# Even layer: attention work in turns beside the in2 linear, the five-tap convolution on its tiles

## The chip, the cores and the metric

One NeuronCore of a Trainium2 chip runs the whole program. The metric is device microseconds for one execution; the median of three runs of the kernel before is 4711.61 us (4707.65 to 4717.33). PE is the tensor engine, DVE the vector engine, ACT the scalar engine, POOL is GpSimd, and SP issues most of the DMAs.

## The reference

The program is a block of two parts over 256 tokens of 2048 features. The first part (a convolution and state-space mixer, a cross attention, an expert layer) is not touched. The second part has an even and an odd layer; the change is in the even one:

```
def even_layer(x, mem, rel_table, norm_g, w_in, conv_w, ..., w_out, lambda_init):
    h = rms_norm_2(x, norm_g) @ w_in
    gq, gk, gv, gb, ga, gg, dq, dk, dv, dg, mq, mg = split_cols(h, EV_SPLITS)
    y = concatenate([
        gdn_branch(gq, gk, gv, gb, ga, gg, conv_w, a_log, dt_bias, gdn_gain),
        diff_attention(dq, dk, dv, dg, rel_table, dq_gain, dk_gain, lam, subln, lambda_init),
        memory_attention(mq, mg, mem, mem_norm, mem_w_kv, mem_qn, mem_kn)])
    return x + y @ w_out
```

- `gdn_branch`: gq, gk and gv (1024 features each) go through a centred convolution of five taps along the tokens and a silu; q and k are normed a head; gb and ga (16 columns each, "the narrow product") give the gates; then a gated delta rule in both directions, a norm and a silu gate.
- `diff_attention`: 8 heads, each with two maps of 64 features. Both maps are normed for q and k, scored with a relative bias, and softmaxed; the second, times a learned lambda, is taken off the first; the result meets dv (128 a head), is normed with `subln` and gated by silu(dg).
- `memory_attention`: 4 heads of 128 over 256 memory rows with normed q and k and a silu gate.

None of the branches depends on another. All is fp32.

## The kernel before

Activations lie feature-major: a tile is 128 features by 256 tokens, x is 16 such chunks. A `Stage` is one block of code for all engines, with its own tiles and semaphores; between stages the engines meet. When few semaphores are free a stage first clears the used ones (`MOST_SEMS` is the reserve).

Weights stream through one ring of four slots for the whole program (`WeightRing`): a piece is 512 KB, 256 input rows by 512 output columns. SP issues piece g when piece g - 4 has been split; the last act of a linear in SP's queue is to load the next linear's first four. `linear` (line 413) goes over tiles of 512 outputs, and in a tile over 8 pieces. For each piece ACT makes the leading part of the fp32 weights (line 394), DVE the trailing part (line 399), and PE does 24 matmuls of 256 columns: leading weights by both parts of the features, trailing weights by the leading part (line 494). ACT may only write a slot of the leading tile when PE has freed it four pieces ago. After a tile, DVE evicts its 4 x 256 columns (lines 544 to 556). The loop over tiles is a hardware loop where a tile has 8 pieces; out2 and out3, of 10 pieces a tile, are written out.

The even layer (line 2336) runs in this order, stage after stage: linear att2 (64 pieces: q, k, gate of the difference attention, q and gate of the memory attention), linear dv2 (16 pieces), `narrow` (line 1892), `write_bias_rows` (line 1939: 8 rows of the bias go to memory), head norms of the memory keys and queries (`head_norm`, line 644: squares on ACT, sums on PE, inverse root on ACT and DVE, spreading over the partitions on PE, product on DVE), memory attention (`attention`, line 1155), head norms of the difference queries and keys, `load_bias` (line 1964: the bias is read back from memory as 8 falling grids of 384 columns and turned by PE), `difference_weight` (line 2305: lambda), difference attention, its head norm and gate, then linear in2 (64 pieces, into `proj`, 32 chunks), and the delta rule (line 2285), which begins with `centered_conv` (line 2004). That one has POOL copy the 24 chunks into a tile with zero columns at both ends, five DVE instructions a chunk (one a tap, four chunks side by side), and a silu on ACT for every four chunks. The memory keys and values were made in the first part and are fetched during att2.

Of the kernel before, what the change touches and what calls it, by code (L numbers as in the profile page):

```python
# [9 lines left out]
P = 128  # L10
# [30 lines left out]
def pieces_of_two_pi():  # L41
# [34 lines left out]
    ("upto", 2 * P), ("before", 2 * P), ("levels", 2 * LEVELS * P), ("round", 1),  # L76
# [26 lines left out]
class Stage:  # L103
# [3 lines left out]
    MOST_SEMS = 40  # L107
# [305 lines left out]
def linear(k, ring, src, dst, residual=False, tokens=False, parts=None, norm=None, fetch=None):  # L413
# [10 lines left out]
    with Stage(nc, f"lin_{name}") as s:  # L424
# [12 lines left out]
        if norm and tokens:  # L437
            col, turned, upright = s.sb("col", [P, TILES]), s.sem("turned"), s.sem("upright")

# [11 lines left out]
        def tile_list(eng):  # L451

            yield 0, 0
            if summing and tiles > 1:
                yield 1, 1
                yield from tile_pairs(eng, tiles, 2) if loops else ((n, n % 2) for n in range(2, tiles))
                return
            yield from tile_pairs(eng, tiles, 1) if loops else ((n, n % 2) for n in range(1, tiles))

        with s.block() as block:  # L460
            @block.sync
            def _(sp):
                if fetch:
                    for to, found in fetch[1]:
                        sp.dma_start(to[:], found).then_inc(fetch[0], 16)
                ring.rest(sp, job)

            @block.tensor
            def _(pe):
                if norm and tokens:  # L470
                    for t in range(TILES):
                        mm = nc.tensor.transpose(acc[:, 1, t, 0:P], norm.scale[:, t * P:(t + 1) * P], k.const("ident"))
                    mm.then_inc(turned, 1)
                for n, half in tile_list(pe):

                    pe.wait_ge(taken, n + 1)
                    for c in range(per):
# [19 lines left out]
                        if first_tile(n) and summing:  # L497
# [4 lines left out]
                            mm.then_inc(summed, 1)  # L502

            @block.scalar
            def _(act):
                for n, _ in tile_list(act):
                    for c in range(per):
# [21 lines left out]
                        if second_tile(n) and summing and c == min(1, per - 1):  # L529
                            inverse.on_scalar(act)  # L530

            @block.vector
            def _(dve):
                v = nc.vector

                def take(n, half):
# [12 lines left out]
                    out = dst[:, bass.ds(n * 4, 4) if not isinstance(n, int) else slice(n * 4, n * 4 + 4)]  # L549
                    if residual:  # L550
# [14 lines left out]
                if summing:  # L565
                    ch = Chain(dve, step)
                for n, half in tile_list(dve):
                    for c in range(per):
# [20 lines left out]
                        if not first_tile(n) and c == min(3 if summing else 1, per - 1):  # L589
                            take(n - 1, 1 - half)  # L590
                take(tiles - 1, (tiles - 1) % 2)

# [734 lines left out]

def cross_attention(k, ring, h, y, key, value):
# [674 lines left out]
def centered_conv(k, x):  # L2004

    nc = k.nc

    chunks, pad, side = 24, (GDN_CONV - 1) // 2, 4
    with Stage(nc, "conv5") as s:
        wide = s.sb("wide", [P, chunks, SEQ + 2 * pad])  # L2010
        step, done, moved = s.sem("step"), s.sem("done"), s.sem("moved")
        weights = k.col("ev_conv")
        with s.block() as block:
            @block.scalar
            def _(act):
                with act.Fori(0, chunks // side) as i:
                    act.wait_ge(done, i + 1)
                    here = x[:, bass.ds(i * side, side)]
                    nc.scalar.activation(here, here, ACT.Silu)

            @block.gpsimd
            def _(pool):
                nc.gpsimd.memset(wide[:, :, 0:pad], 0.0)
                nc.gpsimd.memset(wide[:, :, pad + SEQ:], 0.0)
                for c in range(0, chunks, side):
                    nc.gpsimd.tensor_copy(wide[:, c:c + side, pad:pad + SEQ], x[:, c:c + side]).then_inc(moved, 1)

            @block.vector
            def _(dve):
                ch = Chain(dve, step)  # L2030
                for i in ch.loop(chunks // side, GDN_CONV):

                    dve.wait_ge(moved, i + 1)
                    for tap in range(GDN_CONV):
                        for c in range(side):
                            here = x[:, bass.ds(i * side + c, 1)]
# [661 lines left out]
```

## Time and profile before

| | us |
|---|---|
| median of three runs | 4711.61 |
| profiled execution, time | 4704.41 |
| profiled execution, span | 4702.8 |
| small stages between dv2 and in2 | 218.2 |
| in2 linear | 191.3 |
| five-tap convolution | 62.2 |

A row of a timeline gives the start and the duration in us, engine, line, what is written from what, the number of instructions merged in it, and in brackets the idle time before it with what ended it. A matmul of fp32 operands stands as two records, one of the split parts as one; a record's printed duration overlaps the next one, so its pace is the distance of starts, or a merged row's duration by its count. The granted clock is a share of 2.4 GHz: 1.00 is that, 0.50 is 1.2 GHz, and a value between is a mean over a stretch that had both.

### The profile page before, as it was taken

The numbers are of one execution on the slowest core, as the hardware profiler recorded it, in microseconds if no ns is written. First come the engines' busy times: TensorE is split into PE (matmuls) and PEld (weight loads), VectorE is DVE, ScalarE is ACT, GpSimd is POOL, SyncE is SP. The second block draws the span as 40 slices with busy tenths as digits, with TensorE's granted clock in tenths as the row PEclk, the third lists the DMA queues.
The fourth block names the chain that finished last, engine by engine and source line by source line (L and its number), as shares of the span: only waits on it lengthen the run. The fifth ranks groups of instructions, "written<-read, shape, count | busy, mean of one in ns | idle before, by whom it ended". The sixth has DMA issues, their size and how long they took to land. (4 is left out here: it accounts for less than half of the span.)

```text
span 4702.8 us, 67077 instructions
## 1 busy us (share of the span) xinstructions
PE 4060.8 (86%) x24872; PEld 3592.4 (76%) x24872; DVE 2591.6 (55%) x3882; ACT 1634.9 (35%) x2075; POOL 53.1 (1%) x99
## 2 busy tenths in 40 slices
PE   7878789988589999999999989866946879997679
PEld 7864489974478888888888879746946779997569
DVE  4578654448865655655655655334455554543534
ACT  3214333330244444444444433223311123431333
POOL 0002000000000000000000000000000000000000
PEclk9989899989899999999999999867968989998779
DMA  6333344533356656656656535302510004553104
GB/s 214 120 101 121 103 148 140 158 107 117 125 196 209 206 184 213 205 187 209 205 189 209 187 131 188 126 14 68 183 36 1 0 32 163 180 182 111 37 25 164
DMA packets 181929, 645.74 MB, mean 137 GB/s; under 512 B 24744, under 2 KB 27048, under 8 KB 179888
## 3 DMA queue, kind: packets, MB, share of 16 engines
q1 hardware_dynamic: 173328, 620.56, 39.9%
q0 software_dynamic: 2016, 19.92, 1.1%
q8 instruction: 169, 2.77, 0.2%
q10 hardware_dynamic: 6336, 1.84, 0.2%
q14 instruction: 80, 0.66, 0.0%
HBM read 621.26 MB, written 20.99 MB: 137 GB/s over the span
## 5 line engine op out<-in xcount | busy, mean ns | idle before, releaser
L1813 DVE TENSOR_TENSOR dense_weights_trailing<-weight_ring,dense_weights_leading 128x1024 fp32r<-128x1024 f32 x512 | 624.2, 1225 | 557.2 <-ACT dense_weights_leading L1777 556.4
L1777 ACT ACTIVATE dense_weights_leading<-weight_ring 128x1024 fp32r<-128x1024 f32 x512 | 538.5, 1058 | 679.8 <-PE dense_down L1767 351.5
L1745 PE MATMUL dense_up<-pe_parts,dense_weights_leading 128*128 128x512 f32 x2048 | 720.0, 399 | 21.1 <-DVE dense_weights_trailing L1813 14.7
L1767 PE MATMUL dense_down<-dense_weights_leading,dense_act_parts 128*128 128x512 f32 x2048 | 630.4, 389 | 0.0
L1745 PE MATMUL dense_up<-pe_parts,dense_weights_trailing 128*128 128x256 f32 x2048 | 552.6, 280 | 0.0
L494 PE MATMUL lin_in_acc<-lin_in_parts,lin_in_weights_leading 128*128 128x256 f32 x2432 | 445.6, 286 | 30.5 <-DVE lin_in_weights_trailing L399 30.5
L1745 PEld LDWEIGHTS dense_up<-pe_parts,dense_weights_leading 128*128 128x128 f32 x2048 | 378.8, 188 | 113.5 <-issue 18.9
L1767 PEld LDWEIGHTS dense_down<-dense_weights_leading,dense_act_parts 128*128 128x128 f32 x2048 | 384.5, 188 | 79.2
L399 DVE TENSOR_TENSOR lin_in_weights_trailing<-weight_ring,lin_in_weights_leading 128x1024 fp32r<-128x1024 f32 x216 | 263.2, 1224 | 266.2 <-ACT lin_in_weights_leading L394 266.2
L494 PEld LDWEIGHTS lin_in_acc<-lin_in_parts,lin_in_weights_leading 128*128 128x128 f32 x2432 | 383.9, 194 | 31.5 <-issue 30.6
L1767 PE MATMUL dense_down<-dense_weights_trailing,dense_act_parts 128*128 128x512 f32 x1024 | 398.3, 389 | 0.0
L1745 PEld LDWEIGHTS dense_up<-pe_parts,dense_weights_trailing 128*128 128x128 f32 x2048 | 387.1, 189 | 10.1
L494 PE MATMUL lin_out_acc<-lin_out_parts,lin_out_weights_leading 128*128 128x256 f32 x1792 | 327.7, 286 | 26.1 <-DVE lin_out_weights_trailing L399 26.1
L394 ACT ACTIVATE lin_in_weights_leading<-weight_ring 128x1024 fp32r<-128x1024 f32 x216 | 227.6, 1057 | 343.3 <-PE lin_in_acc L494 341.3
L494 PE MATMUL lin_in_acc<-lin_in_parts,lin_in_weights_trailing 128*128 128x256 f32 x1216 | 346.0, 285 | 0.0
L494 PEld LDWEIGHTS lin_out_acc<-lin_out_parts,lin_out_weights_leading 128*128 128x128 f32 x1792 | 283.7, 195 | 27.1 <-issue 27.1
L494 PE MATMUL lin_out_acc<-lin_out_parts,lin_out_weights_trailing 128*128 128x256 f32 x896 | 255.7, 285 | 0.0
L494 PEld LDWEIGHTS lin_in_acc<-lin_in_parts,lin_in_weights_trailing 128*128 128x128 f32 x1216 | 235.3, 194 | 0.0
L1767 PEld LDWEIGHTS dense_down<-dense_weights_trailing,dense_act_parts 128*128 128x128 f32 x1024 | 192.2, 188 | 40.2
L494 PE MATMUL lin_att_acc<-ev_parts,lin_att_weights_leading 128*128 128x256 f32 x1024 | 188.1, 286 | 14.5 <-DVE lin_att_weights_trailing L399 14.5
L399 DVE TENSOR_TENSOR lin_out_weights_trailing<-weight_ring,lin_out_weights_leading 128x1024 fp32r<-128x1024 f32 x112 | 136.4, 1224 | 114.5 <-ACT lin_out_weights_leading L394 114.5
L494 PE MATMUL lin_in_acc<-ev_parts,lin_in_weights_leading 128*128 128x256 f32 x1024 | 187.0, 286 | 10.3 <-DVE lin_in_weights_trailing L399 10.3
(600 smaller groups left out, 6780.6 us busy)
## 6 DMA issues: line engine op xcount, KB each, us to landing
weight_ring<-in_w_experts SPq DMA_DIRECT2D x512, 512.0 KB, 4.0
weight_ring<-in_w_in SPq DMA_DIRECT2D x216, 512.0 KB, 4.1
weight_ring<-in_w_out SPq DMA_DIRECT2D x112, 512.0 KB, 4.3
weight_ring<-in_w_att SPq DMA_DIRECT2D x64, 512.0 KB, 4.3
weight_ring<-in_w_key SPq DMA_DIRECT2D x32, 512.0 KB, 3.5
weight_ring<-in_w_value SPq DMA_DIRECT2D x32, 512.0 KB, 3.5
weight_ring<-in_w_query SPq DMA_DIRECT2D x32, 512.0 KB, 4.2
weight_ring<-in_w_o SPq DMA_DIRECT2D x32, 512.0 KB, 4.3
```

The lines of the kernel that those rows point to most:

```text
L394: self.nc.scalar.activation(leading, x, ACT.Copy).then_inc(self.led, 1)
L399: return self.nc.vector.tensor_tensor(trailing, x, leading.bitcast(F32), ALU.subtract)
L494: mm = nc.tensor.matmul(acc[:, half, sub], still, moving, start=begin and m == 0, stop=end and m == 2, skip_group_check=not tokens)
L1745: mm = nc.tensor.matmul(to, still, moving, start=begin and m == 0, stop=end and m == 1)
L1767: mm = nc.tensor.matmul(down[:, bank, t], still, moving, start=begin and m == 0, stop=end and m == 2)
L1777: nc.scalar.activation(ring.leading[:, b], ring.ring[:, b], ACT.Copy).then_inc(split_led, 1)
L1813: v.tensor_tensor(ring.trailing[:, b], ring.ring[:, b], ring.leading[:, b].bitcast(F32), ALU.subtract).then_inc(ring.split, 1)
```

## The change

In words:
- The stages between dv2 and in2 are gone but for `write_bias_rows` and `difference_weight`, which now follow each other. Their work is in a class `EvenBeside`, which `linear` takes as `beside` for in2. Each engine has a generator of turns. After each of the 64 pieces PE takes one turn; ACT and DVE, which split four pieces ahead, take turn i after their part of piece i + 4. The loop over tiles is written out.
- PE's turns in order: narrow product, bias grids and sums of squares (turns 1 to 6), spreading of 12 groups of two chunks (9 to 14), memory attention (15 to 23), difference attention (24 to 51, three turns a head), the last norm (53, 54, 57, 58).
- DVE has a second generator, `finish`: the convolution of a tile of in2, one tap (four instructions) after each of five pieces in eight, from piece 12. The first six tiles are evicted into 4 chunks of x and the convolution writes `proj`; the edge columns are left out instead of padded. ACT's silus of these tiles are its last turns.
- x is needed for room (bias, raw tile): it goes to memory in two DMAs of 1 MB during dv2 and comes back during the delta rule's second head norm.
- In turns, a norm's scale is spread a head at a time from one column broadcast over 128 or 64 columns, not from a tile of broadcast copies.
- The bias is read during in2 by one DMA of SP's queue ahead of the ring's; the narrow weights are fetched in att2 on SP's queue, not on ACT's in their own stage.
- The masks of the delta rule (2 x 7 x 128 columns) are no longer part of the constants loaded at the start; they are loaded in the delta rule's first head norm, and the second waits for them.
- `MOST_SEMS` goes from 40 to 60. The columns of att2 stand in another order.

The diff, cut to its core (the classes that are new are quoted where the order or a wait matters):

```diff
-    MOST_SEMS = 40
+    MOST_SEMS = 60
...
 def linear(..., fetch=None, beside=None):
+        other = beside(s) if beside else None
...
+            if other:
+                yield from ((n, n % 2) for n in range(1, tiles))
+                return
...  (SP)
+                if other:
+                    other.on_sync(sp)
                 ring.rest(sp, job)
...  (PE, after each piece)
+                        if other:
+                            next(turns, None)
...  (ACT, after each piece)
+                        if other and n * per + c >= slots:
+                            next(turns, None)
...  (DVE, after each piece)
+                        if other:
+                            if not first_tile(n) and c == slots:
+                                take(n - 1, 1 - half)
+                            if n * per + c >= slots:
+                                next(turns, None)
+                            if n * per + c >= slots + per:
+                                next(finishing, None)
...
+class NormsBeside:
+    def square(self, act, g):
+        if g >= 2:
+            act.wait_ge(self.summed, g - 1)
+        activation(self.sq[:, g % 2], self.groups[g][0], ACT.Square).then_inc(self.squared, 1)
+    def spread_out(self, pe, g):
+        if g >= 2:
+            pe.wait_ge(self.applied, g - 1)
+        for c, t, at in self.columns(g):
+            for h in range(heads):
+                mm = matmul(self.rows[h * wide:(h + 1) * wide, g % 2, ...],
+                            self.scale[:, at + h:at + h + 1].to_broadcast([P, wide]), ident)
...
+class AttentionBeside:
+        self.turn_lag, self.turn_part = {1: (3, 0), 2: (1, 1), 3: (1, 1)}[step]
+        self.value_lag = {1: 5, 2: 2, 3: 2}[step]
+    def turns(self):
+        for i in range(self.heads + self.value_lag):
+            for part in range(self.step if i < self.heads + self.value_lag - 1 else 1):
+                yield i, part
...  (PE)
+        for i, part in self.turns():
+            if i < self.heads and part < maps:
+                scores(i * maps + part)        # waits for most() of two units before
+            if part == self.turn_part and 0 <= i - self.turn_lag < self.heads:
+                turn(i - self.turn_lag)        # waits for normalize()
+            if part == 0 and 0 <= i - self.value_lag:
+                values(i - self.value_lag)     # waits for ACT's copy
+            yield
...  (ACT: raise_unit in parts 1 and 2, copy in part 1)
...  (DVE)
+            if i < self.heads and part < maps:
+                most(i * maps + part)
+            elif i < self.heads and part == self.step - 1:
+                for c in range(maps):
+                    normalize(i * maps + c)
+            if part == 0 and 0 <= i - self.value_lag:
+                take(i - self.value_lag)
...
+class EvenBeside:
+    CONVOLVED = 6
+    def finish(self, dve, taken):
+        for n in range(self.CONVOLVED):
+            dve.wait_ge(taken, n + 3)
+            for tap in (pad, *(x for x in range(GDN_CONV) if x != pad)):
+                for j in range(4):
+                    if tap == pad:
+                        ins = v.tensor_scalar(self.proj[:, c], self.raw[:, j], w, None, ALU.mult)
+                    else:
+                        ins = v.scalar_tensor_tensor(out=self.proj[:, c, to], in0=self.raw[:, j, seen], ...)
+                ch.then(ins)
+                yield
+            yield from idle(3)
...
-def centered_conv(k, x):
...
 def delta_rule(k, proj, ba, spare, out, back):
-        centered_conv(k, proj)
-        head_norm(k, q, 8, 1, 1, GDN_DK ** -0.5)
-        head_norm(k, kk, 8, 1, 1, 1.0)
+        head_norm(k, q, ..., fetch=(masks_here, [... k.args["levels"] in two halves ...]))
+        head_norm(k, kk, 8, 1, 1, 1.0, here=masks_here, fetch=back)
...
 def even_layer(k, ring):
-            narrow(...); write_bias_rows(k, scratch); head_norm x2; attention(memory)
-            head_norm x2; load_bias; difference_weight; attention(difference); head_norm; gate_by_silu
-        linear(k, ring, k.x, proj, parts=parts, norm=norm)
+            linear(k, ring, k.x, att, ..., fetch=(mem_here, found + [narrow_w]))
+            linear(k, ring, k.x, dv, tokens=True, ..., fetch=(x_out, [(spilled[:, h], k.x[:, h]) for h in halves]))
+            write_bias_rows(k, scratch)
+            difference_weight(k, lam, subln)
+            linear(k, ring, k.x, proj, parts=parts, norm=norm, beside=lambda s: EvenBeside(...))
```

## Rows read from the trace of the kernel before

**Rows 1.** The page: its head and first section (busy us, share of span, instructions).
```profile
span 4702.8 us, 67077 instructions
PE 4060.8 (86%) x24872; PEld 3592.4 (76%) x24872; DVE 2591.6 (55%) x3882; ACT 1634.9 (35%) x2075; POOL 53.1 (1%) x99
```

**Rows 2.** Stretches, dv to delta: length, busy PE, PEld, DVE, ACT, POOL; clock, DMA.
```profile
3029.60:3048.50 18.90, 14.27 (x66) 13.93 (x66) 1.26 (x4) 0.00 (x0) 0.00 (x0) 0.55 0.09 14
3048.50:3054.50 6.00, 1.87 (x2) 0.10 (x2) 0.68 (x1) 0.00 (x0) 0.00 (x0) 0.50 0.02 3
3054.50:3146.20 91.70, 59.34 (x252) 49.63 (x252) 29.20 (x62) 18.59 (x40) 0.00 (x0) 0.66 0.05 18
3146.20:3148.50 2.30, 0.00 (x0) 0.00 (x0) 0.95 (x5) 1.49 (x2) 0.00 (x0) 0.77 0.00 0
3148.50:3224.40 75.90, 37.55 (x128) 25.65 (x128) 43.58 (x128) 22.25 (x72) 0.00 (x0) 0.62 0.00 1
3224.40:3247.80 23.40, 13.19 (x64) 12.91 (x64) 6.48 (x12) 6.97 (x9) 0.00 (x0) 0.61 0.00 0
3247.80:3439.10 191.30, 187.21 (x1536) 187.03 (x1536) 86.68 (x72) 67.44 (x64) 0.00 (x0) 0.98 0.54 176
3439.10:3501.30 62.20, 0.00 (x0) 0.00 (x0) 50.61 (x120) 6.34 (x6) 6.33 (x8) 0.52 0.00 0
```

**Rows 3.** Timeline: in2's first matmuls (at low clock), in2's and out2's splits on ACT.
```profile
3251.35 0.63 PE L494 MATMUL lin_in_acc<-ev_parts,lin_in_weights_leading 128*128 128x256 f32 x2
3251.99 0.63 PE L494 MATMUL lin_in_acc<-ev_parts,lin_in_weights_leading 128*128 128x256 f32 x2
...
3265.08 1.06 ACT L394 ACTIVATE lin_in_weights_leading<-weight_ring 128x1024 fp32r<-128x1024 f32 x1 [1.82 <-PE lin_in_acc L494]
...
3906.52 1.06 ACT L394 ACTIVATE lin_out_weights_leading<-weight_ring 128x1024 fp32r<-128x1024 f32 x1 [1.82 <-PE lin_out_acc L494]
```

**Rows 4.** Timeline of PE: records of fp32 matmuls and transposes in several stages.
```profile
805.32 10.60 PE L1196 MATMUL attn_score<-one_key,one_h 128*128 128x256 f32 x48 [1.65 <-PEq L460]
815.76 0.60 PE L1206 MATMUL attn_turned<-consts,attn_probs 128*128 128x128 f32 x4
816.19 3.62 PE L1196 MATMUL attn_score<-one_key,one_h 128*128 128x256 f32 x16
...
3033.93 13.86 PE L1919 MATMUL narrow_got<-narrow_w,x 128*128 128x32 f32 x64 [3.56 <-DVE narrow_w L1926]
...
3501.99 6.99 PE L688 MATMUL hnorm_sums<-consts,hnorm_sq 128*128 128x1 f32 x32 [64.22 <-ACT hnorm_sq L677]
...
3554.81 1.95 PE L2135 MATMUL delta_ps_c<-ev_proj 128*128 128x128 f32 x16
```

**Rows 5.** Stretches, columns as in rows 2: end of an attention; the delta stage.
```profile
830.00:840.00 10.00, 5.40 (x27) 4.48 (x27) 4.97 (x6) 3.44 (x5) 0.00 (x0) 1.00 0.00 0
3570.00:3600.00 30.00, 28.07 (x227) 27.31 (x225) 19.37 (x31) 5.96 (x10) 0.00 (x0) 0.93 0.00 1
```

**Rows 6.** Timeline of DVE: one difference head, first to last; convolution taps.
```profile
3172.17 0.76 DVE L1277 SCALAR_TENSOR_TENSOR attn_biased<-attn_score,ev_bias 128x256 f32<-128x256 f32 x2 [4.24 <-PE attn_score L1196]
...
3177.46 0.42 DVE L1315 COPY ev_y<-attn_got 128x256 f32<-128x256 f32 x1
...
3453.55 1.21 DVE L2040 TENSOR_SCALAR ev_proj<-conv_wide,cols  x4 [0.81 <-DVE ev_proj L2042]
3454.94 1.67 DVE L2042 SCALAR_TENSOR_TENSOR ev_proj<-conv_wide,cols,ev_proj  x4 [0.18 <-DVE ev_proj L2040]
3456.79 1.67 DVE L2042 SCALAR_TENSOR_TENSOR ev_proj<-conv_wide,cols,ev_proj  x4 [0.18 <-DVE ev_proj L2042]
```

**Rows 7.** DMA issues with KB each and median us from issue to landing; timeline of SP.
```profile
4.21 0.49 SPq L304 DMA_DIRECT2D consts<-in_consts  x1
...
consts<-in_consts SPq DMA_DIRECT2D x1, 2177.0 KB, 15.2
...
ev_y<-bias_rows SPq DMA_DIRECT2D x1, 1536.0 KB, 6.3
```

**Rows 8.** Timeline of ACT: a table load ahead of a silu.
```profile
3242.96 1.28 ACT L735 ACT_TABLE_LOAD   x1 [10.59 <-PEq L120]
```

More of the change, by code:

```diff
@@ L410, in __init__, with linear @@
         self.gain, self.scale, self.made = gain, scale, made
[L413 removed]
+def linear(k, ring, src, dst, residual=False, tokens=False, parts=None, norm=None, fetch=None, beside=None):
     nc = k.nc
@@ L473, in _ @@
                     mm.then_inc(turned, 1)
+                turns = other.on_tensor(pe) if other else None
                 for n, half in tile_list(pe):
@@ L530, in _ @@
                             inverse.on_scalar(act)
+                        if other and n * per + c >= slots:
+                            next(turns, None)
+                if other:
+                    for _ in turns:
+                        pass
             @block.vector
@@ L566, in _ @@
                     ch = Chain(dve, step)
+                if other:
+                    turns, finishing = other.on_vector(dve), other.finish(dve, taken)
                 for n, half in tile_list(dve):
@@ L588, in _ @@
                                 inverse.refine(dve, ch, norm.scale[:], scaled)
-                        if not first_tile(n) and c == min(3 if summing else 1, per - 1):
+                        if other:
+                            if not first_tile(n) and c == slots:
[4 more added lines that the diff above has]
+                                next(finishing, None)
+                        elif not first_tile(n) and c == min(3 if summing else 1, per - 1):
                             take(n - 1, 1 - half)
+                if other:
+                    for _ in range(slots):
+                        next(turns, None)
+                        next(finishing, None)
                 take(tiles - 1, (tiles - 1) % 2)
+                if other:
+                    for _ in turns:
+                        pass
+                    for _ in finishing:
+                        pass
 class LinearBeside:
@@ L2001, in _ @@
                     ins.then_inc(taken, 1)
-def centered_conv(k, x):
[L2006 to L2036, printed above, removed]
-                            seen = wide[:, bass.ds(i * side + c, 1), tap:tap + SEQ]
-                            w = weights[:, bass.ds((i * side + c) * GDN_CONV + tap, 1)]
-                            if tap == 0:
-                                ins = nc.vector.tensor_scalar(here, seen, w, None, ALU.mult)
-                            else:
-                                ins = nc.vector.scalar_tensor_tensor(out=here, in0=seen, scalar=w, in1=here,
-                                                                     op0=ALU.mult, op1=ALU.add)
-                        ch.then(ins)
-                    dve.sem_inc(done, 1)
 def delta_gates(k, ba, beta, log_decay):
@@ L2282, in _, with delta_rule @@
                     v.tensor_copy(state[:], ps_b[:])
-def delta_rule(k, proj, ba, spare, out):
+def delta_rule(k, proj, ba, spare, out, back):
     nc = k.nc
@@ L2372, in even_layer @@
+            norm.made = True
+            linear(k, ring, k.x, dv, tokens=True, parts=parts, norm=norm,
+                   fetch=(x_out, [(spilled[:, h], k.x[:, h]) for h in halves]))
+            write_bias_rows(k, scratch)
+            difference_weight(k, lam, subln)
+            linear(k, ring, k.x, proj, parts=parts, norm=norm, beside=lambda s: EvenBeside(
+                k, s, norm, narrow_w, ba, att, dv, proj, mem_here, x_out, scratch, lam, subln))
         features.close()
         with nc.sbuf_tensor("ev_spare", [P, 2 * DC, SEQ], F32, side="right") as spare:
-            delta_rule(k, proj, ba, spare, y[:, 0:8])
```

431 lines of the change are left out of this document (400 added, 31 removed).

## The prediction

> **What bounds the kernel now.** I read the page's first section, then one table over the stretches of the even layer, then the timelines of PE, ACT and DVE inside them. By the page PE is busy 86% of 4702.8 us and DVE 55% [rows 1]. The table shows where PE is not what ends the time [rows 2]: between the dv linear (last eviction before 3029.6) and the in2 linear (from 3247.8) stand 218.2 us of small stages, one after another. There the clock granted to PE is between 0.50 and 0.77 and DVE is busy 82 us in all. Then in2 takes 191.3 us with PE busy 187.2, DVE 86.7 and ACT 67.4; then the five-tap convolution takes 62.2 us with DVE busy 50.6 and PE idle. So in2 is bound by PE, with DVE free 104 us and ACT 124 us beside it, and around it stand 280 us in which PE does little. In in2 every piece of weights comes 1.06 + 1.82 = 2.88 us after the last, the wait being for PE [rows 3]: 64 pieces are 184.3 us and the stage adds 7.0 (first splits, a start at 1.2 GHz, last eviction).
>
> **What is removed from the path.**
> 1. Of the 218.2 us only the bias rows (6.0) and the lambda stage (2.3) stay where they are [rows 2]. 218.2 - 8.3 = 209.9 us leave. Nothing covers them now.
> 2. The convolution's own stage: 62.2 us [rows 2], with GpSimd's copies into a padded tile. The new one reads the unpadded tile and leaves the edge columns out.
> 3. The masks (2 x 7 x 128 columns of 4 B on 128 partitions, 896 KB) no longer come with the constants. Of 6758 KB loaded ahead of the first linear (x, columns, four weight pieces, constants, rows) the constants of 2177 KB land 15.2 us after their issue at 4.21 [rows 7]. Landing began at 1 us or so, so 19 us carry some 6600 KB: 347 KB a us, 2.6 us for 896 KB. I take 2.4, ends 0 and 3.
>
> Together 274.5 us.
>
> **What is added to in2.** The loop over pieces is written out, and after each piece each engine takes one turn of the other work. Writing out costs nothing by the out2 linear, which is written out already and has the same 1.06 + 1.82 [rows 3].
>
> PE prices at 2.4 GHz: 48 records of 256 fp32 columns take 10.60, 0.22 each; four transposes take 816.19 - 815.76 = 0.43; a record of 128 columns 1.95 / 16 = 0.12 [rows 4]. Records with few moving columns stand there only at a low clock (64 in 13.86 at 0.55, 32 in 6.99), 0.217 each; I take half, 0.11, ends 0.10 and 0.217.
> - A, pieces 0 to 23 (narrow product, bias, 12 norm groups, memory attention): narrow 64 x 0.11 = 7.0; 8 flips of 384 columns in 16 records of 0.33 = 5.3; sums 12 groups x 8 x 0.11 = 10.6; spreading 4 groups x 8 x 0.12 = 3.8, and 8 groups with two heads a chunk, which is twice as many, 8 x 16 x 0.12 = 15.4; four heads of 8 x 0.22 + 0.43 = 8.8; transposes 0.3. Sum 51.2; with 24 x 2.88 = 69.1 it is 120.3.
> - B, pieces 24 to 51 (28 turns, eight difference heads, three turns a head): 8 x (12 x 0.22 + 0.43) = 24.6, with 28 x 2.88 = 80.6 it is 105.2.
> - C, pieces 52 to 63 (last norm): 32 x 0.11 + 32 x 0.12 = 7.4, with 34.6 it is 42.0.
>
> DVE in the same three. A split or an eviction is 86.68 / 72 = 1.20 [rows 2]. A difference head costs 3177.46 + 0.42 - 3172.17 = 5.71 with its small gaps; a convolution tap over four chunks costs 1.67 + 0.18 = 1.85, the first of a tile 1.21 + 0.18 = 1.39 [rows 6].
> - A: splits and evictions (28 + 3) x 1.20 = 37, narrow 1.3, norms, bias and memory attention at most 29.2 (4.6 of which, the broadcast scales, go), ten taps 18: 86, below PE's 120.
> - B: (28 + 4) x 1.20 = 38.4, heads 8 x 5.71 = 45.7, nineteen taps 4 x 1.39 + 15 x 1.85 = 33.3: 117.4, above PE's 105.2. **Here DVE takes over as the bound.**
> - C: far below PE.
>
> ACT has 67.4 + 18.6 + 22.3 + 7.0 + 6.3 [rows 2], some 122 us with all it takes over, and some five table loads of 1.28 [rows 8]; in every phase it is below both others. Linear: 120.3 + 117.4 + 42.0 + 7.0 = 286.7, which is 95.4 more than 191.3.
>
> **Edits that I cost at nothing**, each with its cover. x goes out to memory (2 MB) during the dv linear, ahead of that linear's fifth piece in SP's queue: 1536 KB took 6.3 us [rows 7] and PE holds four pieces (11 us); without the cover up to 5 us. x comes back (2 MB) behind a later head norm and is wanted 250 us later. The bias read (1536 KB, 6.3 us) stands in SP's queue before in2's fifth piece and is wanted after PE's fourth, 20 us on. The narrow weights move from ACT's queue to SP's, before the att2 linear's fifth piece. The masks load during a head norm (such a norm and a gate took 23.4 together [rows 2]), the next norm waits for them: at the rate above 896 KB are 2.6 us. The higher semaphore reserve moves or adds clearings, the stage count falls: -3 to +3.
>
> **Clock.** B leaves PE idle a tenth of the time in short waits. 10 us with PE busy 5.4 were granted 1.00; 30 us of the delta stage, full of short waits, 0.93 [rows 5]. I take 1.00; at 0.93 throughout B, PE needs 113, still below DVE.
> The Trainium skill, "TensorE: Matmul & The Clock Gate", section "HAM oscillation — how this bites in real kernels", speaks against the change: an array that waits for others between bursts is put back to the low clock, again and again. The rows at 1.00 and 0.93 don't bear this out for waits this short; where it held, the time would be the third rival's.
>
> **Sum.** -274.5 + 95.4 = -179.1. The profiled execution took 4704.4 (span 4702.8): 4525.3. The median shown is 4711.6, 7.2 above it: **4532.5**.
>
> **Rivals.**
> - Round trip. One piece frees a slot, ACT splits (1.06), DVE splits (1.20), DVE takes its turn (in B 1.7 and a tap of 1.85), and only then may PE's turn go on: if PE's next turn wanted that very result, a piece of B would cost 1.06 + 1.20 + 3.55 + 0.9 + 2.88, 9.6 less the tap, 7.7 us, and B 216 instead of 117: 4631. Against: the turns are laid so that PE wants what DVE made two turns before (turn(h) one head late, values two). For: three engines each run their turns in written order, so any one wait is passed on. At a quarter of the pieces it is +25. The Trainium skill, "TensorE: Matmul & The Clock Gate", section "Architectural detail: the array is 16× 32×32, not 1× 128×128", says that ACT and DVE take their queues strictly in order; if so nothing slips past a waiting turn, and its time is that of this rival. No row here shows one overtaking.
> - All hidden under PE: B at PE's 105.2 and a start four pieces ahead, the 192 few-column records at 0.10: 12 + 4 + 2 less, 4514.
> - Slower than before: the low clock in the whole of in2. At 1.2 GHz three records take 3251.99 - 3251.35 = 0.64 [rows 3], a piece 5.12, 64 pieces 328; the other work's 83.2 doubles to 166; with 4.5 around it 499, added 307 against 274.5 removed: 4744. It decides from 465.8 us for in2, 7.3 a piece. For: small stages now run at 0.5 to 0.6. Against: in2's own matmuls fill 184 of the 287 us and the other work 83, and the clocks of [rows 5].
> - The other work doesn't run beside but at the end (turns left over when the pieces are out): by the counts, 59 turns on PE and DVE against 64 pieces, it doesn't.
>
> **How the numbers follow.** Forecast 0.70 (within 20 us of its sum), round trip 0.13 at more than +45, hidden 0.13, low clock 0.03, no effect 0.01. Ends of the unknown costs: few-column records at 0.217 add 192 x 0.107 = 21, queues 5, clearings 3, waits between turns up to 30; below, 18 and the 3 of clearings, 7 of run to run. Range 4500 to 4592. About 0.2% (9 us) is what a measurement can tell from no change: faster 0.96, within 0.01, slower 0.03.
>
> **What would show it.** In the trace after: no rows of small stages between dv and in2 but bias rows and lambda; in2 some 287 us long; pieces 2.88 apart when a turn is empty, near 5 in A, near 4.2 in B, where DVE is busy over 90% and PE waits on DVE; 2.9 again at the end; granted clock 1.00; the head norm of the delta part starts right after in2; the first linear starts 2.4 earlier. Wrong if pieces in B stand 6 or more apart with DVE idle too, if the clock in in2 falls to 0.5 for tens of us, or if PE waits for weights at the dv linear's fifth piece.

## The result, and the profile after

The changed kernel takes 4522.4 us (median of 4 runs, 4512.7 to 4526.3), against 4709.6 for the one before, measured beside it: ratio 0.960, with a 95% interval of 0.9585 to 0.9614. Measured twice more, it took 4525.4 and 4525.3 (5 runs each). The forecast was 4532.5. The profiled execution took 4519.8 us, 184.6 less than that of before; the forecast was 179.1 less.

The page's head and first section, for [rows 1]:
```profile
span 4518.2 us, 66715 instructions
...
PE 4025.7 (89%) x24940; PEld 3565.1 (79%) x24940; DVE 2574.8 (57%) x3873; ACT 1631.9 (36%) x2072; POOL 46.7 (1%) x91
```
The engines' busy times fall by 35 us (PE), 17 (DVE) and 3 (ACT). Next to no work is gone: 149.5 of the 184.6 us are time in which PE stood idle, and most of PE's 35 is the work of the small stages, whose records took 126 us at a granted clock of 0.50 to 0.77 ([rows 2]) and take 88 us in in2. Timelines of DVE, PE and ACT from the end of the dv linear to the start of the delta part (start, us, engine, line, what, count, idle before and what ended it):
```profile
3028.24 1.41 DVE L566 TENSOR_SCALAR ev_dv<-lin_dv_acc,lin_dv_col 128x512 f32<-128x512 f32 x2 [8.50 <-PE lin_dv_acc L505]
3031.43 1.45 PE L2460 MATMUL bias_got<-consts,bias_table 32*8 32x512 f32 x2 [3.24 <-DMA bias_table<-in_rel_bias]
...
3037.27 0.15 DVE L2785 TENSOR_SCALAR ev_lam<-ev_lam 128x1 f32<-128x1 f32 x1
3037.83 3.90 ACT L394 ACTIVATE lin_in_weights_leading<-weight_ring 128x1024 fp32r<-128x1024 f32 x4 [0.78 <-PEq L2775]
...
3314.12 1.22 DVE L580 TENSOR_TENSOR ev_proj<-ev_scale,lin_in_acc 128x1024 f32<-128x1024 f32 x1 [9.13 <-PE lin_in_acc L505]
3317.35 1.67 ACT L719 ACTIVATE hnorm_sq<-ev_proj 128x512 f32<-128x512 f32 x3 [9.83 <-PEq L120]
```
The dv linear ends at 3029.65, as before (3029.6 in [rows 2]; that it is so near may be chance, see below). Bias rows and lambda take 8.0 us, in2 277.7 (3037.6 to 3315.3), then a clearing of semaphores (L120) 2.0, and the delta part's head norm begins at 3317.3 instead of 3501.3. All but 0.6 of the gain is in this stretch.

The three phases of in2, to be set beside [rows 2] (length, busy PE, PEld, DVE, ACT, POOL with counts; granted clock, DMA share, GB/s):
```profile
3037.60:3161.20 123.60, 120.41 (x963) 115.79 (x964) 71.11 (x123) 47.27 (x65) 0.00 (x0) 0.93 0.38 126
3161.20:3271.70 110.50, 110.50 (x802) 101.31 (x801) 104.74 (x228) 49.85 (x101) 0.00 (x0) 1.00 0.39 130
3271.70:3315.40 43.70, 42.16 (x353) 41.71 (x351) 25.35 (x39) 21.46 (x24) 0.00 (x0) 1.00 0.37 126
```
A, B and C are the forecast's three phases: pieces 0 to 23, 24 to 51 and 52 to 63. PE is busy all of the 110.5 us of phase B, DVE 104.7 of them (95%). This is all that PE waits for in in2, by the view of waits (engine, its tile and line, what it waits for: us, times, longest):
```profile
PE lin_in_acc L505 <- DVE lin_in_weights_trailing L399: 7.4, 1, 7.4
PE lin_in_beside L1513 <- DVE ev_att L1606: 0.5, 1, 0.5
PE lin_in_beside L1429 <- DVE ev_att L1438: 0.2, 1, 0.2
```
The first is the start of the stage, most of it under the bias and lambda stages. Behind it PE waits 0.7 us in 275.

### The profile page after: what moved, and what is told of

Same layout as the page of the kernel before. It is cut to its first block and busy times, and to the rows that moved or that the text cites. A ratio compares the mean times of both kernels' runs of the same rounds, so it can differ in the third digit from the quotient of the medians.

```text
span 4518.2 us, 66715 instructions
## 1 busy us (share of the span) xinstructions
PE 4025.7 (89%) x24940; PEld 3565.1 (79%) x24940; DVE 2574.8 (57%) x3873; ACT 1631.9 (36%) x2072; POOL 46.7 (1%) x91
## 5 line engine op out<-in xcount | busy, mean ns | idle before, releaser
L2249 PEld LDWEIGHTS dense_up<-pe_parts,dense_weights_leading 128*128 128x128 f32 x2048 | 379.3, 189 | 114.0 <-issue 18.5
L505 PE MATMUL lin_in_acc<-ev_parts,lin_in_weights_leading 128*128 128x256 f32 x1024 | 196.3, 293 | 7.4 <-DVE lin_in_weights_trailing L399 7.4
```

The source lines that it names most:

```text
L505: mm = nc.tensor.matmul(acc[:, half, sub], still, moving, start=begin and m == 0, stop=end and m == 2, skip_group_check=not tokens)
L2249: mm = nc.tensor.matmul(to, still, moving, start=begin and m == 0, stop=end and m == 1)
```

## The experiments

**The reserve of semaphores alone.** The kernel before with the new reserve:
```
-    MOST_SEMS = 40
+    MOST_SEMS = 60
```

> The kernel before with one edit: the semaphore reserve of a stage is 60 and not 40, so that used semaphores are cleared at other stage boundaries. In the changed kernel the first linear starts 2.6 us earlier, but at the end of the dv linear nothing is left of it: 3029.65 against 3029.57. Theory (the reserve): the places of the clearings move, one to just ahead of the expert choice, where GpSimd's staging of the keys is on the path; here the end of the dv linear then stands 2 to 3 us later than in the kernel before (3032), and the total is 2 to 4 us more. Rival (the new DMAs in att2 and dv, or the smaller constants, cost it): this kernel is as before, within 1 us at the end of the dv linear.

Measured: 4699.1 us (10 runs, 4692.8 to 4703.3) against 4708.4 (13 runs, 4703.2 to 4718.6), ratio 0.9978 with an interval of 0.9969 to 0.9988: faster by 9.3, well under 2% but clear of noise, which no theory had. The dv linear ends at 3033.0, 3.4 later than before, near what the theory said (though executions of one code differ by as much there, see the part on the constants below), but the total isn't longer: the profiled execution is 1.1 shorter than that of before. The four clearings have moved (the first from 1198 to 995 us, the last from 4573 to 4388), and the two traces, laid over each other, drift apart by up to some 6.8 us around 3220 and end 1.1 apart. The pair can't show the 9 us anyway: this profiled execution (4703.3) is among the slowest of its ten, and that of before (4704.4) is 7.2 under its median. Where the 9 us lie stays open. The other way round:

**The old reserve in the new kernel**, 60 only where in2 opens:
```
-        if self.nc.free_len() < self.MOST_SEMS:
+        if self.nc.free_len() < self.reserve:      # 60 for in2, 40 elsewhere
```

> The kernel after, with the reserve of semaphores at 60 only where the new in2 stage opens and at 40 (as in the kernel before) everywhere else, so that the clearings fall elsewhere. The trace shows that with 60 one clearing now stands ahead of the top-k scores (the 2.6 us won at the start are gone by there). Theory: the places of the clearings move the time by no more than 3 us either way. Rival, from the kernel before with 60 (its median 9.3 us below before's, its profiled execution only 1.1 below): the reserve of 60 is worth about 9 us by itself, and this kernel comes out 5 to 10 us slower than after.

Measured: 4524.9 against 4525.4 for the changed kernel beside it. In the new kernel the clearings' places are worth nothing that shows in the total. Whether some of the 187 us between the medians is the reserve's in the kernel before stays open; it is 9 at most, and the two profiled executions, which differ by 184.6, don't need it.

**The convolution in its own stage again**, all else as changed:
```
-    CONVOLVED = 6
+    CONVOLVED = 0
...
+        centered_conv(k, proj)
```

> The changed kernel with one part undone: the five-tap convolution is again a stage of its own behind the in2 linear, with its padded tile and GpSimd's copies; all eight tiles of in2 are evicted straight to proj. Theory (PE bounds in2 throughout, DVE stands at 95% in the 28 pieces with the difference attention): the convolution costs in2 nothing, in2 stays at 278 us within 1.5, and the total is the stage's 62 more, some 4584. Rival (DVE, or DVE and PE in turn, set the pace of those pieces, as forecast): without 17 taps there in2 falls to PE's own sum, 5 us less, total some 4579.

Measured: 4587.0 us, 62 to 65 above the changed kernel's medians. Phases of in2 and the convolution's stage behind it, columns as above:
```profile
3042.70:3168.57 125.87, 122.97 (x963) 118.53 (x964) 56.21 (x83) 47.26 (x65) 0.00 (x0) 0.90 0.36 124
3168.57:3279.07 110.50, 110.50 (x802) 101.35 (x801) 80.83 (x160) 49.23 (x101) 0.00 (x0) 1.00 0.39 132
3279.07:3322.70 43.63, 42.11 (x353) 41.66 (x351) 20.08 (x26) 15.72 (x18) 0.00 (x0) 1.00 0.36 121
3322.70:3387.20 64.50, 0.00 (x0) 0.00 (x0) 50.60 (x120) 6.99 (x8) 6.33 (x8) 0.53 0.00 0
```
This is the clearest reading of the study. B is 110.50 us long with 80.8 us of DVE work in it and 110.50 with 104.7: DVE's load doesn't set its length, and the convolution lies in in2 for nothing. The last row has the clearing of semaphores (2.0) in front and the first 0.65 us of the head norm at its end; the convolution itself takes 61.9. Moved in, it takes these off and adds none.

**Two more taps per tile on DVE** (multiplied by zero, so that the result stays), in place of two empty turns:
```
-            for tap in (pad, *(x for x in range(GDN_CONV) if x != pad)):
+            for tap in (pad, 0, None, None, 1, 3, 4):      # None: four operations with scalar 0.0
...
-            yield from idle(3)
+            yield from idle(1)
```

> The changed kernel with more work on DVE: each tile's convolution gets two more taps of four instructions that add nothing, 1.66 us each, seven pieces of eight instead of five. In the 28 pieces of the difference attention that is 7 taps, 11.6 us, on top of 104.7 busy of 110.5. Theory (PE bounds now, DVE has 5.8 us left there): DVE needs 116.3, in2 grows by some 6 (4 to 9), total some 4528, and PE now waits for DVE. Rival (DVE is the bound already): in2 grows by 11.6 or more, 4534. Second rival (DVE has slack from running four pieces ahead): under 2.

Measured: 4533.7 us (4528.1 to 4534.8), 11.3 above the changed kernel's first median, 8.3 above the later ones; in2 is 12.7 longer. Of these 4.8 are low clock, 3.1 of it in phase A, where it differs from execution to execution (below); 7.9 are left, inside the theory's 4 to 9. PE's waits for the heads come to nearly the same, by the view of waits:
```profile
PE lin_in_beside L1501 <- DVE lin_in_probs L1592: 8.3, 5, 4.1
```
The timeline of PE, the first score records of four heads and one wait between them:
```profile
3205.62 1.13 PE L1491 MATMUL lin_in_beside<-ev_att 64*128 64x256 f32 x4
3217.99 1.13 PE L1491 MATMUL lin_in_beside<-ev_att 64*128 64x256 f32 x4
...
3231.33 1.13 PE L1491 MATMUL lin_in_beside<-ev_att 64*128 64x256 f32 x4
...
3238.88 0.66 PE L1501 MATMUL lin_in_beside<-consts,lin_in_probs 128*128 128x128 f32 x4 [1.44 <-DVE lin_in_probs L1592]
3245.21 1.13 PE L1491 MATMUL lin_in_beside<-ev_att 64*128 64x256 f32 x4
```
The fourth and fifth head are 12.37 apart, as in the changed kernel, then 13.34 and 13.88: DVE's slack is spent after these, and only then does PE wait for the probabilities. So DVE was near the bound, as its 95% says, but on the other side of it; in all of in2, 16.6 us of added DVE work cost some 8. The longest wait (4.1 us, up to 3279.9) is followed by 3.4 us at 1.2 GHz, from 3281.1 on.

**Transposes one turn earlier** (a head has three turns, parts 0 to 2), which shortens the way from DVE to PE:
```
-        self.turn_lag, self.turn_part = {1: (3, 0), 2: (1, 1), 3: (1, 1)}[step]
+        self.turn_lag, self.turn_part = {1: (3, 0), 2: (1, 1), 3: (1, 0)}[step]
```

> The changed kernel with one lag shortened: in the difference attention PE transposes a head's probabilities, and ACT copies them, in part 0 of the next head's turns instead of part 1, so that PE wants in turn j + 1 what DVE makes in turn j. Theory (the lags of two turns are what keeps the round trip off the path): from the freeing of a slot DVE is done with its turn after 1.06 + 1.2 + 2.3 = 4.6 us at the earliest, PE is there after 2.9; 1.7 us a head, with DVE at 95% rather more: in2 grows by 10 to 30, 4533 to 4552. Rival (the engines' lead of four pieces hides it anyway): under 2 us.

Measured: 4539.7 us, in2 288.7 from its first matmul to its last eviction instead of 275.1. PE's waits for the heads:
```profile
PE lin_in_beside L1501 <- DVE lin_in_probs L1592: 11.4, 8, 1.8
```
Phase B:
```profile
3159.62:3282.00 122.38, 110.96 (x790) 101.19 (x789) 104.99 (x228) 49.48 (x100) 0.00 (x0) 0.99 0.35 116
```
All eight heads wait, 1.4 us on the mean and 1.8 at most: the round trip of the first rival is real, and the chosen lags keep the kernel clear of it. In2 is 13.6 us longer, 1.6 of them low clock (one fall to 1.2 GHz, 3.4 us long, comes right behind the first head's wait of 1.8), so the round trip costs 12.0, not the hundred of the rival's worst case, since it binds once a head and not once a piece.

**The clock.** Phase A has 0.93 where 1.00 was forecast. Stretches of it in the changed kernel:
```profile
3044.00:3052.00 8.00, 8.00 (x64) 7.80 (x62) 3.12 (x4) 3.16 (x4) 0.00 (x0) 0.90 0.78 304
3052.00:3059.00 7.00, 7.00 (x36) 7.00 (x36) 0.00 (x0) 1.26 (x2) 0.00 (x0) 0.53 0.22 75
3059.00:3066.00 7.00, 7.00 (x63) 7.00 (x63) 1.64 (x3) 1.98 (x3) 0.00 (x0) 0.99 0.23 75
3066.00:3069.00 3.00, 3.00 (x17) 3.00 (x16) 0.00 (x0) 0.33 (x1) 0.00 (x0) 0.51 0.03 5
```
and PE's few-column work there:
```profile
3048.79 3.79 PE L1714 MATMUL lin_in_beside<-ev_narrow,x 128*128 128x32 f32 x32
3052.39 3.55 PE L1400 MATMUL lin_in_beside<-consts,lin_in_sq_biased 128*128 128x1 f32 x16
3060.25 3.66 PE L1714 MATMUL lin_in_beside<-ev_narrow,x 128*128 128x32 f32 x32
...
3071.25 1.84 PE L1400 MATMUL lin_in_beside<-consts,lin_in_sq_biased 128*128 128x2 f32 x16
```
Below, "low clock" is one minus the granted clock summed from in2's first matmul to its last eviction, so that 2 us at 1.2 GHz count as 1 us lost. It costs 7.8 us in this execution, 2.6 of them at the start and 5.1 in the two dips. The Trainium skill, "TensorE: Matmul & The Clock Gate", section "HAM oscillation — how this bites in real kernels", knows the fall of the clock from an array that stands idle between bursts; here the rows show it with PE's records filling 7.00 of 7.00 us, behind matmuls of few columns. Three more kernels and two repeats look into it.

Four lots of 16 instead of two of 32:
```
-            if turn <= TILES:
-                t = turn - 1
-                for c in range(DC):
+            if turn <= 2 * TILES:
+                t, part = divmod(turn - 1, 2)
+                for c in range(part * DC // 2, (part + 1) * DC // 2):
```

> The kernel after, with the narrow product's 64 matmuls of 32 columns issued in four lots of 16 (turns 1 to 4) instead of two lots of 32 (turns 1 and 2), the flips and the rest of that piece's schedule two turns later; the same work in all. In the trace of after the granted clock falls from 1.00 to 0.50 right after each lot of 32 plus 16 one-column sums (3052.3 to 3058.9 us, again 3066.1 to 3068.9), which costs about 5.1 us of in2's first phase (2 us slices: sum of 1 minus the clock, times 2). Theory: it is the long run of few-column work that takes the clock down, so with half lots in2 gets 3 to 5 us shorter (274.5 -> 270 to 272 from its first matmul to its last eviction) and the kernel about 4 us faster than after. Rival 1: the clock dips after each lot all the same, four short dips instead of two: no change within 1 us, or up to 3 us slower. Rival 2: the dips have nothing to do with the narrow product: they stay where they are in time, no change.

Measured: 4523.9 against 4525.4. In its trace four dips follow the four lots, together with the start 12.5 us of low clock: the first rival's picture. (The kernel below with the same lots and the lambda stage merged has three dips and 10.3 us.)

Eight lots of 8, each between quarters of a piece (`within` holds the same matmuls, four instructions at a time):
```
+                            if other and sub < 3 and 2 <= n * per + c <= 4:
+                                next(lots, None)
```

> The kernel after with the same 64 records in eight lots of 8 (0.9 us each at the full clock), put between the quarters of pieces 2 to 4, each lot with a quarter of a piece (0.7 us and more of 256-column matmuls) on both sides, away from the sums; the flips two turns later as in the kernel with four lots. Theory: the clock falls when few-column work makes up most of some microseconds; lots as short as that don't do it, or hardly: in2 268 to 271 us. Rival: pieces 2 to 4 as a whole are now half few-column work, and the clock falls over all of them: in2 276 to 284 us.

Measured: 4533.3 us, 8.0 above the changed kernel beside it; in2 is 289.7 us long, where the theory had 268 to 271 and the rival 276 to 284: the theory is refuted, and it is worse than the rival said. The stretches from 4 us into in2 on:
```profile
3049.00:3055.00 6.00, 6.00 (x49) 5.78 (x49) 2.89 (x3) 3.85 (x6) 0.00 (x0) 0.96 0.91 337
3055.00:3095.00 40.00, 40.00 (x195) 40.00 (x195) 4.23 (x7) 7.52 (x10) 0.00 (x0) 0.52 0.17 56
```
The timeline of PE, the first two lots:
```profile
3055.55 1.01 PE L1709 MATMUL lin_in_beside<-ev_narrow,x 128*128 128x32 f32 x8
...
3057.80 1.75 PE L1709 MATMUL lin_in_beside<-ev_narrow,x 128*128 128x32 f32 x8
```
The clock fell at the end of the first lot (which follows sixteen sums of one column) and stayed at 1.2 GHz from 3056.3 to 3097.3, 41 us without a break, with PE busy all of them; the last lot ends 10 us before it rises, and the sums stand between the pieces all along. Of the three ways to issue this work, the eight lots mixed into the pieces are clearly the worst; two and four lots aren't told apart (5.1, 8.5 and 10.2 us of dips in three executions against 8.5 and 10.2 in two).

All but the first chunk of the narrow product left out:
```
-                for c in range(DC):
+                for c in range(1):
```

> The kernel after without 60 of the 64 records of 32 columns: of each sequence tile's narrow product only the first chunk is computed (so the gates' inputs ba are incomplete), everything else in place. Theory, after four half lots brought four dips of the clock instead of two: the dips are these matmuls' doing, the sixteen one-column sums alone don't bring any. Then in2 loses the lots' own 2 times 3.6 us and the dips (5.1 us in after, 8.5 us in the second execution of after), and is 263 to 266 us long instead of 275 to 278. Rival: the sums alone bring the clock down as well, the dips stay and in2 is 268 to 271 us.

Measured: 4515.9 us, 9.4 under the changed kernel beside it; in2 265.1 from first matmul to last eviction. The kernel leaves the gates' inputs incomplete, so it is no variant to use. Low clock is 4.1 us, 1.7 of which is one short dip (3056 to 3059) behind the first sums of one column and the four narrow records that are left. The theory's length is met; its claim that no dip is left without the lots is not. That the lots bring most of the dips is shown by this run.

The lambda stage merged into the bias rows' stage, with the four lots and with the eight:
```
+                ch.then(v.tensor_tensor(prod[:], lam[:, :, 0], lam[:, :, 1], ALU.mult))
+                v.tensor_reduce(dots[:], prod[:], AX.X, ALU.add).then_inc(ready, 1)
...
-            difference_weight(k, lam, subln)
```

> The kernel after with the spread narrow product and with the lambda stage merged into the bias rows' stage (its six small operations beside the bias rows' transfer instead of behind it; a stage's own cost less). In after's trace the lambda stage goes from 3035.5 to 3037.4 us, so 1.5 to 2.5 us go with it. Theory: 4522.4 less 4 less 2, about 4516.5. Rival: the spreading is worth nothing, 4520.5.

> The eight lots and the lambda stage merged into the bias rows' stage. With the theory of the lots 4522 less 6 less 2, about 4514; with its rival about 4522.

Measured: 4522.6 us (4515.4 to 4524.2) with four lots, 4536.2 with eight. Both are slower than either theory said (4516.5 or 4520.5, and 4514 or 4522). From the dv linear's last eviction to in2's first matmul it is 8.7 and 8.9 us instead of the 10.6 to 11.2 of the unmerged kernels: the merge is worth some 2 us, as it promised. With four lots this is the fastest kernel of the study that computes everything, by 2.8 us in medians of 5 beside the changed kernel; the two sets of runs overlap, so no more than a likely small gain.

The changed kernel itself, once beside each of the two groups of kernels above:

> The kernel after itself, unchanged, as the measure for the three beside it: 4522 within 5 us, and in its trace in2 274 to 276 us long from first matmul to last eviction. If its median or in2's length is off by more, differences of that size between the others are not told apart.

> The kernel after unchanged, beside the three others: 4524 within 4 us, in2 275 to 278 us; a third look at how long the two dips of the clock are in one execution (5.1 and 8.5 us so far).

Measured: 4525.4 and 4525.3 us, in2 278.1 and 280.5 from first matmul to last eviction, low clock 10.6 and 12.6. The table sets length against low clock (us, from first matmul to last eviction):

| kernel | in2 | low clock | difference |
|---|---|---|---|
| changed, three executions | 275.1, 278.1, 280.5 | 7.8, 10.6, 12.6 | 267.3, 267.4, 267.9 |
| old reserve outside in2 | 278.3 | 10.7 | 267.6 |
| convolution in its own stage | 277.2 | 10.7 | 266.6 |
| four lots | 279.9 | 12.5 | 267.4 |
| four lots, lambda merged | 278.5 | 10.3 | 268.2 |
| eight lots | 289.7 | 22.9 | 266.8 |
| eight lots, lambda merged | 291.2 | 23.8 | 267.5 |
| without the narrow product | 265.1 | 4.1 | 261.0 |
| two more taps | 287.8 | 12.5 | 275.2 |
| transposes earlier | 288.7 | 9.4 | 279.3 |

The difference is the same (266.6 to 268.2) wherever PE's work is the same and nothing is late, and in the last two rows it is longer by about what PE waits (8.3 and 11.4 us). So in the changed kernel in2 is PE's work and its clock and next to nothing else, and most of the spread between its executions (5.4 us here, 4.8 of it low clock) is how long the low clock lasts.

## Why the prediction was right, step by step

The range holds the result and the main claim is right: the small stages and the convolution vanish beside in2, and what in2 grows by is far less. That the sum comes within 10 us is in part luck. Its bound for phase B is the wrong engine's, 6.9 too long, and errors of both signs cancel in phase A. By the total alone the rival "All hidden under PE" (4514) is as near as the forecast (4532.5).

- *Removed from the path, 274.5.* Right in its large parts: no small stage but bias rows and lambda is left (8.0 us, forecast 8.3), and the convolution's stage is gone; put back, it takes 61.9 (62.2 by [rows 2]).
- *Constants at the start, 2.4.* Gained at the start; whether it reaches the end can't be told. The constants land 13.5 us after their issue instead of 15.2 ([rows 7]), and the first table load stands at 18.4 instead of 21.1, and between 18.2 and 18.5 in all executions with the smaller constants. At the end of the dv linear the changed kernel's three executions are at 3029.6, 3031.3 and 3029.2, and the eight others with the new reserve, which run the same code up to there, at 3028.0 to 3034.3: the scatter of 6 us hides the 2.4, and being level with before (3029.6, one execution) may be chance. One wait goes with the reserve: in the memory's top-k part, ahead of which a clearing now stands, PE waits 7.1 to 9.0 us for GpSimd in the twelve executions with the new reserve (8.8 with the reserve alone) and 6.9 in the two with the old one. Against this, the clearing that stood at 1198 before is gone.
- *Phase A, PE 120.3.* Measured 120.9 from the first matmul, by two misses that cancel. Spreading norms of two heads a chunk were priced at 0.12 a record; they take about half:
```profile
3104.17 1.95 PE L1429 MATMUL lin_in_beside<-consts,lin_in_heads_scale 128*128 128x128 f32 x16
3108.92 1.97 PE L1429 MATMUL lin_in_beside<-consts,lin_in_heads_scale 128*64 128x128 f32 x32
```
 so that twice the records cost nearly the same. The records whose stationary operand has 64 columns start in pairs, 0.007 us from each other, and the pairs are 0.11 apart. The four pieces with them are 2.1 longer than an empty one, 8.2 together where 15.4 were forecast: 7.2 less. Against this stands the low clock, 7.8 in this execution and up to 12.6. The few-column record, taken at 0.11 between 0.10 and 0.217, came out at 3.60 / 32 = 0.11 (3048.79 to 3052.39).
- *Phase B: "Here DVE takes over as the bound", 117.4.* **This is the step that failed.** B is 110.5, PE's, as the kernel with the convolution outside shows. DVE is busy over 90% of it, as forecast, but PE never waits for it there. DVE's work is 104.7. Of the 12.7 too many about 3 are the gap of 0.18 behind a tap ([rows 6]), which was read where each tap waits for the last; between other work it mostly goes (five gaps of 0.16 or so, 0.8 together, are left in in2):
```profile
3210.70 1.66 DVE L1693 SCALAR_TENSOR_TENSOR ev_proj<-x,cols,ev_proj 128x255 f32<-128x255 f32 x4
3212.40 1.23 DVE L399 TENSOR_TENSOR lin_in_weights_trailing<-weight_ring,lin_in_weights_leading 128x1024 fp32r<-128x1024 f32 x1
3213.54 0.16 DVE L1586 RECIPROCAL lin_in_diff_inv<-lin_in_diff_total 128x2 f32<-128x2 f32 x1
```
 (3210.70 to 3212.40 is 1.70). Two of the nineteen taps fall outside B (17 x 4 instructions are what B has less with the convolution outside), which is 4. The rest is an estimate: some 2 for the small gaps within a head, and most of what remains for records that overlap by 0.09, as the last two above.
- *Phase B, PE 105.2.* Too little by 5.3. A head is a period of 12.37 us, three pieces of 2.88 and 3.73 of its own instead of 3.07:
```profile
3211.46 1.13 PE L1491 MATMUL lin_in_beside<-ev_att 64*128 64x256 f32 x4
3212.51 1.13 PE L1513 MATMUL lin_in_beside<-lin_in_probs_t,ev_dv 128*128 128x256 f32 x4
3213.29 0.59 PE L505 MATMUL lin_in_acc<-ev_parts,lin_in_weights_leading 128*128 128x256 f32 x2
3213.72 0.28 PE L505 MATMUL lin_in_acc<-ev_parts,lin_in_weights_trailing 128*128 128x256 f32 x1
3213.84 0.40 PE L505 MATMUL lin_in_acc<-ev_parts,lin_in_weights_leading 128*128 128x256 f32 x2
...
3223.82 1.13 PE L1491 MATMUL lin_in_beside<-ev_att 64*128 64x256 f32 x4
```
 The scores' stationary operand has 64 rows (the 64*128 in their rows), all others in this phase have 128. Two pieces, one with four fp32 records of 128 rows behind it and one with four score records alone, show what that makes:
```profile
3156.51 1.03 PE L1513 MATMUL lin_in_beside<-lin_in_probs_t,ev_proj 128*128 128x256 f32 x4
3157.19 0.59 PE L505 MATMUL lin_in_acc<-ev_parts,lin_in_weights_leading 128*128 128x256 f32 x2
3157.61 0.28 PE L505 MATMUL lin_in_acc<-ev_parts,lin_in_weights_trailing 128*128 128x256 f32 x1
...
3160.25 1.03 PE L1513 MATMUL lin_in_beside<-lin_in_probs_t,ev_proj 128*128 128x256 f32 x4
...
3164.08 1.13 PE L1491 MATMUL lin_in_beside<-ev_att 64*128 64x256 f32 x4
...
3168.20 1.13 PE L1491 MATMUL lin_in_beside<-ev_att 64*128 64x256 f32 x4
```
 The first is 3.74 long (3156.51 to 3160.25), an empty piece and 4 x 0.216: the way from split to fp32 matmuls and back costs nothing. The second is 4.12 long (3164.08 to 3168.20), 0.38 more. Inside the group two score records still start 0.216 apart; the extra stands at its ends, 0.19 where the rows go from 128 to 64 and 0.19 where they go back. A head has four such changes, 0.72 with the one ahead of the transposes at 0.15, and that is the 0.66 that were missing (the records themselves are 0.05 cheaper than priced). That it is this change and not another property of the scores is read from the rows, and no run tests it alone.
- *Phase C, 42.0.* Measured 42.4, all PE's.
- *In2, 286.7.* Measured 277.7, 9.0 less: B's bound is 6.9 of these, and the 7.0 for the stage's start and end came out 3.1 smaller (2.7 to the first matmul and 1.2 for the last eviction; the low clock of the start is counted in A), while A and C are 1.0 more. The clearing behind in2 takes 2.0 back.
- *Edits at nothing.* Held for the queues: the att2 and dv linears together, from the first weights' split to the last eviction, take 246.6 us, 247.5 before, with x's 2 MB among their pieces. Held for the written-out loop: empty pieces stay 2.88 apart. A clearing behind in2 costs 2.0, another up to 2.1 in the top-k part; within what was allowed them.
- *Clock 1.00.* Right in B and C, where it was argued; wrong in A, where PE hardly waits. The rival of a low clock had the engine's idleness in mind; what lowers the clock in A comes behind few-column work, and is worth 5 to 10 us here and 20 where the work is mixed badly. Waits may bring it down too: the two kernels in which PE waits for the heads have one dip of 3.4 us each right behind a wait, of 1.8 and of 4.1 us; behind their other waits there is none.
- *Rivals.* "All hidden under PE" (4514) is what happened in kind: B is PE's. It missed by the low clock and the dearer heads. Round trip: absent, 0.7 us of waits; shown to lie one turn away.

## What to carry to other kernels

Small stages in a row cost mostly the waits between engines: work that took 272 us in stages of its own lengthened a linear bound by PE by 86 (191.3 to 277.7), which is PE's own records and their clock. To say which engine bounds a mixed phase, count busy time only: gaps read in a stage where one operation waits for the last don't come along. Leave slack on the engine that hands results to PE: at 95% it was free, with 16.6 us more work it was late in some heads, and a lag shorter by one turn cost 12.0. Before reading a few microseconds between two traces, look at how far executions of the same code lie apart: here 6 us at the end of the dv linear.

## What was not expected of the hardware

- The granted clock fell to 1.2 GHz with PE's records following each other without a gap, behind 32-column fp32 matmuls: the dips behind two lots of 32 cost 5.1, 8.5 and 10.2 us, those behind four of 16 cost 8.5 and 10.2, and with eight of 8 mixed among 256-column matmuls the clock stayed low for 41 us.
- Records whose stationary operand has 64 columns started in pairs, so that one took 0.06 us of PE's time; with 128 columns it was 0.11, the moving one being 128 wide in both.
- A change of the stationary operand between 128 and 64 rows took 0.15 to 0.19 us more; one between split and fp32 matmuls of 128 rows took nothing.
- The same kernel's in2 had 7.8, 10.6 and 12.6 us of low clock in three executions, which is most of the spread of its length.
